# Keys decayed on GpSimd and turned by one-record transposes, bonus sums a unit earlier, in a one-core hybrid decoder block

## What is computed

```python
def rwkv7_time_mix(P, ...):
    ...
    def step(S, inp):
        r_t, w_t, k_t, v_t, a_t, b_t = inp
        Sa = einsum("bhvk,bhk->bhv", S, a_t)
        S = S * w_t + Sa[..., None] * b_t + v_t[..., None] * k_t
        y = einsum("bhvk,bhk->bhv", S, r_t)
        return S, y
    _, y = lax.scan(step, S0, (r, decay, k, v, a_vec, b_vec))
    y = ((y - mean) * rsqrt(var + RW_LN_EPS)) * ln_g + ln_b
    bonus = sum(r * k * r_k, axis=-1) * v
    return (y + bonus) * g
```

## Time and profile before

| what | us |
|---|---|
| median of three executions | 1002.21 |
| the profiled execution | 1002.2 |
| its span, first to last instruction | 1000.2 |
| TensorE busy | 963.4 |
| ACT, DVE, POOL busy | 424.7, 399.7, 375.1 |
| preparation beside the qk and v units | about 117 to 215 |
| triangular systems and their solution | 306 to 355 |
| loop over the chunks | 355 to 401 |

### The profile page before, as it was taken

One profiled execution on the slowest core, in us unless ns is written; L12 is line 12 of the kernel. 1 busy time (PEld: TensorE's weight loads), 2 busy tenths in 40 slices (PEclk: granted clock), 3 DMA queues, 4 the chain that ended last, 5 costly groups with the idle time before them and its releaser, 6 DMA issues.

```text
span 1000.2 us, 15861 instructions
## 1 busy us (share of the span) xinstructions
PE 963.4 (96%) x6791; PEld 796.0 (80%) x6791; DVE 399.7 (40%) x624; ACT 424.7 (42%) x665; POOL 375.1 (37%) x175
## 2 busy tenths in 40 slices
PE   6999999989999988999989999999999999999986
PEld 4885877777879988888868888888888888888865
DVE  4110258777564435137425343443434300101445
ACT  6244354344565335352336444444443421412546
POOL 2441443332224112334433344444444444344260
PEclk9999999999999989999999999999999999999999
DMA  8431433322111000224422333333333332324222
GB/s 256 105 101 43 105 86 83 85 85 65 43 49 39 5 3 3 64 86 135 138 85 64 101 89 106 89 101 100 90 106 87 103 121 90 102 88 126 74 74 85
DMA packets 115067, 86.45 MB, mean 86 GB/s; under 512 B 2821, under 2 KB 99991, under 8 KB 114999
## 3 DMA queue, kind: packets, MB, share of 16 engines
q1 hardware_dynamic: 114808, 85.37, 29.0%
q10 hardware_dynamic: 190, 0.08, 0.0%
HBM read 83.34 MB, written 2.10 MB: 85 GB/s over the span
## 4 chain that ended last, share of the span: by engine, by line
PE 73%; ACT 2%; POOL 2%; issue 1%; DVE 1%; POOLq 0%; DVEq 0%; ACTq 0%
PE bank L508 13%; PE bank L509 13%; PE bank L510 13%; PE bank L552 8%; PE bank L553 8%; PE bank L554 8%; PE bank L777 2%; PE bank L787 2%; PE bank L686 1%; PE bank L701 1%; PE bank L674 1%; PE bank L759 1%; PE bank L748 1%; PE bank L727 1%; POOL pleg_w_lo L488 1%
## 5 line engine op out<-in xcount | busy, mean ns | idle before, releaser
L488 POOL TENSOR_TENSOR w_lo<-raw,w_hi 128x1024 fp32r<-128x1024 f32 x138 | 333.1, 2414 | 530.6 <-ACT w_hi L1022 530.6
L1022 ACT ACTIVATE w_hi<-raw 128x1024 fp32r<-128x1024 f32 x138 | 146.4, 1061 | 364.5 <-issue 213.3
L508 PE MATMUL bank<-hT_hi,w_hi 128*128 128x512 f32 (+1 forms) x736 | 286.7, 390 | 2.0 <-POOL w_lo L488 1.9
L510 PE MATMUL bank<-hT_hi,w_lo 128*128 128x512 f32 (+1 forms) x736 | 283.2, 385 | 0.0
L509 PE MATMUL bank<-hT_lo,w_hi 128*128 128x512 f32 (+1 forms) x736 | 283.0, 385 | 0.0
L508 PEld LDWEIGHTS bank<-hT_hi,w_hi 128*128 128x128 f32 x736 | 138.3, 188 | 31.5 <-issue 2.1
L510 PEld LDWEIGHTS bank<-hT_hi,w_lo 128*128 128x128 f32 x736 | 138.2, 188 | 27.8
L509 PEld LDWEIGHTS bank<-hT_lo,w_hi 128*128 128x128 f32 x736 | 138.3, 188 | 27.3 <-issue 0.7
L1796 DVE SCALAR_TENSOR_TENSOR cbuf<-bank,params,cbuf 128x511 f32<-128x511 f32 x48 | 36.0, 750 | 133.9 <-ACT cbuf L1359 133.9
L552 PE MATMUL bank<-w_hi,g_hi 128*128 128x512 f32 x184 | 71.7, 389 | 0.0
L554 PE MATMUL bank<-w_hi,g_lo 128*128 128x512 f32 x184 | 71.6, 389 | 0.0
(11 more groups left out here) (258 smaller groups left out, 1304.9 us busy)
## 6 DMA issues: line engine op xcount, KB each, us to landing
raw<-in_w_up_dram SPq DMA_DIRECT2D x48, 512.0 KB, 3.8
raw<-in_w_in_dram SPq DMA_DIRECT2D x33, 512.0 KB, 4.0
raw<-in_w_down_dram SPq DMA_DIRECT2D x24, 512.0 KB, 3.7
raw<-in_w_gate_dram SPq DMA_DIRECT2D x16, 512.0 KB, 3.9
raw<-in_w_out_dram SPq DMA_DIRECT2D x8, 512.0 KB, 3.9
raw<-in_w_ple_gate_dram SPq DMA_DIRECT2D x8, 512.0 KB, 3.9
xs<-in_x_dram SPq DMA_DIRECT2D x4, 512.0 KB, 5.2
raw<-in_w_branch_a_dram SPq DMA_DIRECT2D x4, 512.0 KB, 3.4
```

What stands on the lines that cost most here:

```text
L488: nc.gpsimd.tensor_tensor(low(n)[:, :], raw[:, n % RAW_SLOTS, :], high(n)[:, :].bitcast(F32), ALU.subtract).then_inc(*step("pool", ("lo", n)))
L508: nc.tensor.matmul(o, wh, ah, start=first, stop=False)
L510: return nc.tensor.matmul(o, wl, ah, start=False, stop=last)
L1022: nc.scalar.activation(high(u)[:, :], raw[:, u % RAW_SLOTS, :], ACT.Copy) \
```

## The change

- *Keys.* POOL multiplies K and B themselves by the decays, into a new tile `Kd` of 4 KB a partition where `DG` of 2 KB stood: two operations of 128 x 512 a group instead of one. PE then turns `Kd` by 16 transposes a group (one record each) instead of 16 matmuls with the diagonal.
- *Values and output.* Of the 16 matmuls of `Vt`, and of the 64 of `yT`, those whose result goes to partitions 0 to 63 become transposes; the other half stays a matmul with the unit matrix. The two kinds alternate.
- *POOL's order.* `Kd(2)` stands before `masked(4)`, and `Kd(3)` before `masked(5)`.
- *Preparation.* `bonus_sum(p-1)` stands behind unit 3p+1 instead of behind unit 3p+2 and `key_norm(p)`; on DVE `pre_c(p-1)` stands before `pre_b(p)` instead of behind it. The last bonus sum keeps its place.

```diff
-            def decay_diagonals(g):
+            def decayed_keys(g):
                 if g == 0:
                     gp.wait_ge(*done("dve", "preC", NPAIR - 1))
                 else:
                     gp.wait_ge(*done("pe", "BK", g - 1))
                 e = stat[:, ec:ec + 32].rearrange("p (h c) -> p c h", c=NCH)[:, 2 * g:2 * g + 2, :]
-                nc.gpsimd.tensor_tensor(DG[:, :, :, :], stacked("ident64").unsqueeze(1).unsqueeze(1).broadcast_to([P, 2, NPAIR, CH]),
-                    e.unsqueeze(3).broadcast_to([P, 2, NPAIR, CH]), ALU.mult).then_inc(*step("pool", ("DG", g)))
+                for s in range(2):
+                    nc.gpsimd.tensor_tensor(Kd[:, s, :, :], Kb[:, :, 2 * g + s, :, :].rearrange("p h two t -> p h (two t)"),
+                        e[:, s, :].unsqueeze(2).broadcast_to([P, NPAIR, 2 * CH]), ALU.mult).then_inc(*step("pool", ("Kd", g)))
...
                 if i % 3 == 2:
                     key_norm(i // 3)
-                    if i // 3 >= 1:
-                        bonus_sum(i // 3 - 1)
+                if i % 3 == 1 and i // 3 >= 1:
+                    bonus_sum(i // 3 - 1)
...
+            def turned(o, x, q, from_top=True):
+                unit = stacked("ident64")[half(q)]
+                return nc.tensor.transpose(o, x, unit) if from_top else nc.tensor.matmul(o, x, unit, start=True, stop=True)
...
-                            mm = nc.tensor.matmul(o[q][:, n * CH:(n + 1) * CH], keys_and_b(p, q, 2 * g + s),
-                                                  DG[half(q), s, p, :], start=True, stop=True)
+                            mm = turned(o[q][:, n * CH:(n + 1) * CH], Kd[half(q), s, p, :], q)
...
-              head_products(o, lambda s, p, q: Vv[half(q), p, chunk_cols(2 * g + s)],
-                              lambda s, p, q: stacked("ident64")[half(q)], shift=1)
+                            mm = turned(o[half(1 - q), n * CH:(n + 1) * CH], Vv[half(q), p, chunk_cols(2 * g + s)], q, q == 1)
...
-                        mm = nc.tensor.matmul(o[half(q), chunk_cols(c)], KK[half(q), p, chunk_cols(c)],
-                                              stacked("ident64")[half(q)], start=True, stop=True)
+                        mm = turned(o[half(q), chunk_cols(c)], KK[half(q), p, chunk_cols(c)], q, q == 0)
...
                 if p + 1 < NPAIR:
                     pre_a(p + 1)
-                pre_b(p)
                 if p:
                     pre_c(p - 1)
+                pre_b(p)
             pre_c(NPAIR - 1)
```

More of the change, by code:

```diff
@@ L100 @@
 SIGNALS = [
-    "act_DK", "act_BK", "pe_RA", "pe_BK", "pool_XT", "pool_DG", "pool_mask",
+    "act_DK", "act_BK", "pe_RA", "pe_BK", "pool_XT", "pool_Kd", "pool_mask",
     "act_E", "act_U", "act_U1", "act_Vt", "act_Am", "act_Wp", "act_chain", "act_exp", "act_g_hi",
@@ L258, in build @@
         Zs, Zd = at("Zs", 112, [P, 2, NPAIR, CH]), at("Zd", 114, [P, NPAIR, CH])
-        U1, DG = at("U1", 115, [P, 2, NPAIR, CH]), at("DG", 117, [P, 2, NPAIR, CH])
+        U1, Kd = at("U1", 115, [P, 2, NPAIR, CH]), at("Kd", 117, [P, 2, NPAIR, 2 * CH])
         early_a, early_b = at("early_a", 122, [P, 4, SEQ]), at("early_b", 56, [P, 4, SEQ])
@@ L476, in _ @@
                     identities(1)
-                    decay_diagonals(0)
+                    decayed_keys(0)
                     identities(2)
@@ L481, in _ @@
                     masked(1)
[L482 to L486, removed]
+                    decayed_keys(1)
+                    masked(2)
+                    masked(3)
+                    decayed_keys(2)
+                    masked(4)
+                    decayed_keys(3)
+                    masked(5)
+                    masked(6)
+                    masked(7)
                 gp.wait_ge(*done("act", "hi", n))
@@ L715, in _, with head_products @@
             token_units([("v1", s) for s in range(2)], [("vt1", m) for m in range(NT)], hT_hi, hT_lo, 4, 256)
-            def head_products(o, lhs, rhs, shift=0, **flags):
+            def head_products(o, lhs, rhs):
                 for s in range(2):
@@ L726, in head_products @@
                             n = NPAIR * s + p
-                            mm = nc.tensor.matmul(o[half(q ^ shift), n * CH:(n + 1) * CH], lhs(s, p, q), rhs(s, p, q),
+                            mm = nc.tensor.matmul(o[half(q), n * CH:(n + 1) * CH], lhs(s, p, q), rhs(s, p, q),
                                                   start=True, stop=True)
@@ L750, in with_r_and_a @@
                 mm.then_inc(*step("pe", ("RA", c)))
+            def turned(o, x, q, from_top=True):
+                unit = stacked("ident64")[half(q)]
+                return nc.tensor.transpose(o, x, unit) if from_top else nc.tensor.matmul(o, x, unit, start=True, stop=True)
             def tokens_of_keys(g):
-                pe.wait_ge(*done("pool", "DG", g))
+                pe.wait_ge(*done("pool", "Kd", g))
                 o = [begin("BK", g, q) for q in range(2)]
@@ L764, in tokens_of_values @@
                 o = begin("Vt", g)
-                head_products(o, lambda s, p, q: Vv[half(q), p, chunk_cols(2 * g + s)],
-                              lambda s, p, q: stacked("ident64")[half(q)], shift=1).then_inc(*step("pe", ("Vt", g)))
+                for s in range(2):
+                    for p in range(NPAIR):
+                        for q in range(2):
+                            n = NPAIR * s + p
+                            mm = turned(o[half(1 - q), n * CH:(n + 1) * CH], Vv[half(q), p, chunk_cols(2 * g + s)], q, q == 1)
+                mm.then_inc(*step("pe", ("Vt", g)))
             def level_w(g, lv):
```

## The result

The changed kernel takes 1058.18 us (median of 4 runs, 1057.83 to 1058.93) beside 1001.82 for the kernel before on the same chip (4 runs): a ratio of 1.0553 [1.0537, 1.0570]. I had forecast 992.0, with 0.15 on slower, and the range ended at 998.5.

What follows compares the result with a forecast made beforehand. TensorE was busy 963.4 of 1000.2 us, so only its work or waits counted. Keys -10.5, V and y 0, preparation +0.3 made -10.2 on 1002.2: 992.0 us, range 988 to 998.5.

Steps and rivals of the forecast that it cites:

- Half of V and y: V and y: the half with two records sets the pace, so half transposes cost 0; bounds -1.8 to +3.7 us.
- my upper bound of +3.7: V and y: a transpose cannot run beside a matmul, three starts of 0.057 us instead of two over 64 pairs.
- The first rival: V and y: alternating transposes drain the array, 0.35 us a pair, +14.5 us, 1006.5 us in all; chance 0.14.
- the third rival: Preparation: all three bonus sums wait 2.5 us, +5, and +10 more if each halves the clock; 997 to 1007; chance 0.08.
- The keys: The four key groups: cheaper transposes, and at group 2 no wait or clock drop; -1.32, -1.28, -6.6, -1.28, sum -10.5 us.
- The part of POOL's order: Key group 2: making its operand before chunk 4's mask removes a 2.40 us wait and the half clock behind it.
- BK(3): Last key group: z waits for u's eviction, could start at 390.66 instead of 391.94, a gain of 1.28 us.
- The fourth rival: Loop: the clock falls all the same, the wait not its cause; 2.9 us come back, 994.9 us; chance 0.06.
- The preparation: Bonus sums and weight tiles: 2.2 us of waits go, new ones of 1.1, 0.7 and 0.7 come; +0.3 us.
- my bound of 1.7: Preparation: the upper end of its net cost, forecast as -1.1 to +1.7 us.

Runs made afterwards that it cites:

- e3: The changed kernel with all transposes first, then all matmuls, in each group of V and each pair of y; 1000.18 us, ratio 0.9984.
- e1: The changed kernel with all turns of V and y as matmuls again, the rest kept; 995.59 us, ratio 0.9939.
- e2: e1 with the preparation of the kernel before on PE and DVE; 993.34 us, ratio 0.9913.
- e7: The kernel before with POOL's new order alone, diagonals of groups 2 and 3 each one mask sooner; 997.27 us, ratio 0.9947.
- e8: e1 with each bonus sum behind unit 3p+2 again, but ahead of that unit's key norm; 989.34 us, ratio 0.9882.
- run 16: Not a follow-up run: "run" is a verb here, the keys' 16 transposes taking 0.49 us from first start to last.
- e9: e8 with the half transposes put back in V's group 0 alone; 1024.46 us, ratio 1.0224.
- e10: e8 with the half transposes put back in V's groups 1 to 3 alone; 1000.63 us, ratio 0.9982.
- e11: e8 with the half transposes put back in y alone; 1007.47 us, ratio 1.0054.

## Why the prediction was wrong, step by step

**The step that failed** is "Half of V and y ... I cost it at 0", with the sentence that carried it: "As the halves run side by side, the half with two records sets the pace". They stop running side by side as soon as one half transposes. A pair takes 0.427 us against 0.116, also beyond my upper bound of +3.7, which allowed for three starts in a row but for nothing between them. The bound came from rows in which all records are of one kind. The row that I leant on against a drain, a matmul 0.02 us behind ten transposes, was of 128 x 128 tiles, and did not carry over to 64 x 64.

**The first rival** was the right mechanism (a cost at each change of kind) with its price too low, in two ways. The pair costs 0.427 us, not the 0.35 that I took from changes of shape: 64 x (0.427 - 0.116) = 19.9 us at full clock instead of 14.5. And the clock was left out. It makes most of the other 41.6 us of the 61.5: 29.4 in the solve, and 4.7 in y (18.4, where 32 pairs at 0.427 are 13.7); the rest, 7.5, lies nearly all in the loop, which takes 14.8 more where 24 pairs at 0.311 more are 7.5. I had priced the clock in the third rival for waits of PE, and never asked the same of a stretch that is busy but slow. On the rule of the Trainium skill (TensorEngine Tiling, Restrictions and Key Properties) that I cited there: it holds float32 transposes and column tiling to exclude each other, yet in e3 the 64 x 64 transposes run as single records, 0.056 us apart, with the tile 64*64. It ties the drain to a change of tiling mode; the trace gives both kinds the same tile, and no run shows whether a mode changes with the kind. What the runs show is a gap of 0.15 to 0.17 us at each change of kind, about that of a change of tile shape (0.15). I gave that rule 0.14 because one row of another shape spoke against it; with no row for the case itself, it deserved more.

**The keys: -10.5 forecast.** Held in its mechanism. Stage by stage, *to the solve*, *solve* and *loop* together, e1 has 117.0 us, e2 117.8 and before 127.1: -10.1 and -9.3. The group of keys takes 0.64 us against my 0.61. The part of POOL's order, the wait and the clock, 2.4 + 2.9 = 5.3 forecast, is the 4.9 of e7 (5.3 in its loop); the transposes, 4 x 1.3 = 5.2, are 4.1 by the stages of e7 and e2. The missing 1.1 is nearly all at `BK(3)`. There, from `solved_u` to z, it takes 2.84 us in e7 and 2.47 in e1, a gain of 0.4 where I had 1.28 (`BK(1)` gives its 1.28: 2.84 and 1.56). I had z wait for u alone; the profile of e1 has it wait for another eviction of ACT (L1240, of what `with_r_and_a` made):

```profile
382.28 0.71 PE L760 MATMUL bank<-consts,Kd 64*128 64x64 f32 x16
383.83 0.69 PE L855 MATMUL bank<-VU,BK 128*64 128x64 f32 x16 [0.84 <-ACT KA L1240]
```

The fourth rival, a clock that falls in the loop all the same, is out: e1, e2, e3, e7 and e8 show none there. But that the wait of 2.40 us was the only long one, as I wrote there, is wrong: the same trace has one of 2.25 us at 506.58, for `out_w_lo`, with the clock full behind it.

**The preparation: +0.3 forecast, +2.1 measured.** The removed waits are gone as forecast, 2.2 us. The first new wait is 1.03 us for 1.1; the other two are 1.49 each instead of 0.7. That term was a midpoint between 0 and 1.4, on a DVE chain (`pre_c(0)`, then `pre_b(1)`) that I put at 13.8 to 15.8 us. In the kernel after it takes 16.3, from the first of these rows of DVE to the end of the second:

```profile
143.30 0.68 DVE L1564 TENSOR_TENSOR Bo<-bank,Vv 128x512 f32<-128x512 f32 x1
...
158.86 0.75 DVE L1558 SCALAR_TENSOR_TENSOR Sc<-RA,params,KA 128x512 f32<-128x512 f32 x1
```

So the preparation's 2.1 lies a little above my bound of 1.7; the waits make 1.8 of it, and the last 0.3 is not traced. The third rival's other half fell: these waits left the clock full.

Put together, my terms gave -10.2 and the kernel without the alternation is 6.2 us (1001.81 - 995.59) faster: of the missing 4.0 the preparation is 1.8 (2.1 against 0.3), the keys 0.4, and a late halved stretch, told of below, 1.4.

## What to carry to other kernels

Before half of a group of matmuls is replaced by something cheaper, ask whether the two kinds can stand next to each other: here the order of the same instructions was worth 57 us, and a saving of one record a pair could never have paid for a change of kind at 0.15 us. Keep a group of one kind, or leave it. Where a stretch becomes slow, price the clock of what follows as well, above all where many small matmuls follow, as the solve did here; and move a consumer only as far as its producer's chain allows, since the same sum put one unit later (e8) turned a loss of 2 us into a gain of 2.8.

## What the runs showed of the hardware

- *Change of kind.* In 64 x 64 tiles, float32: transpose to transpose 0.056 us, transpose to matmul 0.146 to 0.170, the first matmul's second record 0.107, matmul to transpose 0.149; alternating, 0.427 a pair against 0.116 for two matmuls. The same 0.107 to a second record stands at the start of `V(0)` in e1, behind another tile shape, so by its records a change of kind looks like a change of shape. Only transposes to partitions 0 to 63 ran in these tiles. Transposes of 64 rows and 128 columns (the keys) run 16 in 0.49 us from first start to last.
- *A busy engine can lose its clock and be long in getting it back.* Behind one 3.3 us stretch of alternation the solve ran 65.3 us at half speed instead of 35.8 at full speed, in after and in e9. In the loop, behind the same stretches, the clock was back after 3.4 us (e10), or 3.4 and 6.8 (after). Of transposes the Trainium skill (TensorE: Matmul & The Clock Gate, PE-mode transpose) says that they don't count as busy in the same way; no run here sets that apart from the slowness of the alternation, but it is not enough by itself: e3 has the same transposes, 32 of them in y, and full clock throughout.
- *A late halved stretch that comes and goes.* In e1, e9, e10 and e11 the profile has one more stretch of 6.8 us, between 500 and 536 us, that begins 0.7 to 1.4 us behind the first of two waits for `out_w_lo`. Timeline of PE in e1:

```profile
498.46 0.50 PE L557 MATMUL bank<-out_w_hi,mg_hi 128*128 128x512 f32 x1 [2.25 <-POOL out_w_lo L493]
...
501.69 0.79 PE L557 MATMUL bank<-out_w_hi,mg_hi 128*128 128x512 f32 x1 [1.50 <-POOL out_w_lo L493]
```

  The kernel before, the kernel after, e2, e3, e7 and e8 have the same first wait (2.25 us) and kept the clock in their profiles. The mean clock of single runs is lower by about as much in six of six of e1, four of six of e2, two of five of e7, one of five of e8 and one of eight of e3; where in the run it was low, such a mean does not tell. It is worth 1.4 us (564.4 against 563.0 behind y), and what decides it stays open. So a wait of this length is followed by a halved clock at one time and not at another.
